# Pass two of a fused expert stage starts from the weights that pass one left, two engines' programs of it become loops, and the steps of a channel norm are spread over more slots

## The chip, the cores and the metric

One core of one Trainium2 chip runs the whole program. The metric is device time in microseconds (us) from start to end of one execution. The engines are TensorE (PE, its weight loads PEld), VectorE (DVE), ScalarE (ACT), GpSimd (POOL) and SyncE (SP, which only issues transfers here). Each runs its own program in order; they meet through semaphores only.

## The reference, cut to what matters

One decoder layer for 512 prompt tokens and 32 decode tokens (544 in all), all in float32. The parts that the change touches:

```python
def conv_branch(u_ext, conv_w, conv_b, conv_norm_g):
    c = lax.conv_general_dilated(u_ext, conv_w[:, None, :], (1,), 'VALID', ...) + conv_b
    return jax.nn.silu(rms_norm(c, conv_norm_g))

def peer_ffn(x, w_query, keys1, keys2, expert_u, expert_v):
    ...                    # idx: 16 of 16384 experts for each of 8 heads, g: their softmax
    act = jax.nn.gelu(jnp.einsum('nd,nhkd->nhk', xc, expert_u[idx]), approximate=False)
    return jnp.einsum('nhk,nhkd->nd', g * act, expert_v[idx])
```

Block-sparse attention over paged caches runs beside the convolution. `expert_u` and `expert_v` are 64 MB each.

## The kernel before

The work comes in stages: the input projection, the attention stage (with the convolution's steps between it), the output and query projections, and two passes over the experts.

**Attention stage.** It runs in slots t = 0 to 64. `at = t - 33` counts the slots of its second half, in which TensorE multiplies one chunk of cached values (1 MB) in each slot (`attend`, L1722), for a first batch of four sequences in `at` 0 to 15 and for a second one in 16 to 31. One unit of prompt attention enters in most slots: scores on TensorE (L1635), maximum on VectorE (L1146, L1148), exponent on ScalarE (L803), norm on VectorE (L1155, L1157), transposes and values on TensorE. Before the second batch, TensorE turns that batch's probabilities in five groups (L1709), and ScalarE copies each group out (`keep_probabilities`, L848 and L851), after it has copied the first batch's output (`keep_output`, L857). TensorE waits at its third group for the first copy. The convolution's RMS norm has these steps: root on ScalarE (L704) in `at` 13, reciprocal (L1020) and four scalings (L1269) on VectorE in `at` 14, four sigmoids `sig_c` (L894) on ScalarE in `at` 15, and the products `finish_conv` (L1235 and after) in `at` 17 to 20. Every value chunk has one of four buffers and is loaded again when an `attend` has freed it.

**Weights of the experts.** A product in float32 is made of three matmuls with a high and a low part. For one step of 256 experts a raw 1 MB tile is loaded (SyncE), ScalarE writes its high part (`high_u`, L922) and another engine the low part (`split_u`). There are three places for split tiles: 0 and 1 (`w_hi`, `w_lo`), and 2, the first 256 columns of `x_hi` and `x_lo`, which are free when pass one is over.

**Pass one** (L1828 and after, `up`) goes over 64 steps for the first 256 tokens; GpSimd makes the low parts (L632). Its activations go to memory, from where single ones are fetched later. The gates of the other tokens are made beside it and stored too.

**Pass two, the fused stage.** 68 slots (`ENDS`). In slot s TensorE does `up_beside` for the other 288 tokens (48 matmuls, with expert step s), and from slot 4 on `down` for expert step s - 4 (48 matmuls, L1525 to L1527 with `a_hi`), whose weights v lie in place 1. Its program is straight for eight slots and then a loop of eight. For the first 256 tokens, whose experts are sparse, GpSimd fetches 256 times one activation per token (`fetch_unit`, L649) and 256 times one row of v per token (`fetch_row`, L656), and VectorE adds the rows (`add_row`, L1430); a row has one of six buffers, so that fetch k + 6 waits for `row_used` of add k. In most slots GpSimd makes four such pairs, and in some five. In the middle of them it multiplies the slot's two activation tiles by the gates (`gate_acts`, L644). ScalarE then makes their high part (`high_a`, L977) and after that the high part of v (`high_v`, L970), VectorE the low parts (`low_acts` L1472, `split_v` L1480, `split_u` L1455), in the order of these loops:

```python
                if c >= 0:
                    split_v(c)
                for k in mine[:1]:
                    add_row(k)
                if slot + 1 < STEPS:
                    split_u(STEPS + slot + 1)
                for k in mine[1:4]:
                    add_row(k)
                for step in gated_at(slot):
                    low_acts(step)
```

`gated_at` gives slot 2 the gates of slots 0 and 1, slot 3 those of 2 and 3, and later each slot its own. GpSimd's first unit fetches wait for the last activations of pass one to be stored.

## Time and profile before

| | |
|---|---|
| median of three runs | 1965.66 us (1964.97 to 1965.74) |
| profiled execution | 1983.77 us, its span 1982.3 us |
| attention stage, second half | about 315 to 436 us of the span |
| pass one | about 617 to 1065 us |
| pass two | 1065 us to the end |
| TensorE's clock, mean over the span | 0.964 of full speed |

The profiled execution is 18.1 us longer than the median of the others. Times inside it are counted from the span's start. A releaser behind "<-" is what ended an idle stretch of an engine, by the semaphore events; "issue" is time that the profile lays to no wait.

### The profile page before, as it was taken

Reading aid. Unit: us, or ns where it says so; the run is one execution under the profiler, and the core shown is the slowest. Engines: PE = TensorE matmul, PEld = TensorE weight load, DVE = VectorE, ACT = ScalarE, POOL = GpSimd, SP = SyncE. Lnnn points to the kernel's source line nnn. Section 1 sums busy time; section 2 is a strip of 40 time slices with the busy share of each in tenths; the row PEclk is TensorE's granted clock in tenths of the full one; section 3 lists DMA queues with packets and bytes.
Section 4 is the critical chain, followed back from the end, with each engine's and each line's share of the span. In section 5 each row is a group of like instructions: output and inputs, shape, how many; then the busy total and the mean of one; then the engine's idle time right before and its main releaser. Section 6 shows DMA issues by size and latency. Waiting matters only on the chain.

```text
span 1982.3 us, 38018 instructions
## 1 busy us (share of the span) xinstructions
PE 1844.2 (93%) x14571; PEld 1732.4 (87%) x14571; DVE 1458.1 (74%) x2603; ACT 821.3 (41%) x1103; POOL 1162.8 (59%) x943
## 2 busy tenths in 40 slices
PE   6988988789899999999998899999999999999996
PEld 6977764349899999999998899999998999999985
DVE  3659675431589889857774788888887888888873
ACT  4233764422213545456774434334333444334331
POOL 3232222223234888874466688888887788888840
PEclk9989998889899999999999899999999999999997
DMA  4353877672123676775687799999999899999971
GB/s 158 87 112 120 287 253 260 230 279 84 65 86 120 216 235 218 221 231 218 234 335 274 242 342 343 349 329 335 340 330 340 308 347 346 341 331 345 320 241 67
DMA packets 207753, 491.59 MB, mean 248 GB/s; under 512 B 34209, under 2 KB 119266, under 8 KB 187138
## 3 DMA queue, kind: packets, MB, share of 16 engines
q1 hardware_dynamic: 145906, 319.11, 46.8%
q0 software_dynamic: 55296, 167.94, 23.7%
q10 hardware_dynamic: 6416, 2.78, 1.1%
q8 instruction: 79, 1.29, 0.3%
q14 instruction: 56, 0.46, 0.1%
HBM read 449.10 MB, written 40.66 MB: 247 GB/s over the span
## 4 chain that ended last, share of the span: by engine, by line
PE 46%; POOL 31%; issue 9%; DVE 7%; ACT 5%; DVEq 1%; DMA 1%; another core or an unknown queue 0%; ACTq 0%; POOLq 0%; SPq 0%
POOL v_rows L656 13%; POOL picked_a L649 12%; PE pair L1525 11%; PE pair L1526 11%; PE pair L1527 11%; POOL act L644 5%; PE pair L1858 3%; PE pair L1670 3%; PE pair L1682 1%; PE pair L1722 1%; PE pair L1535 1%; PE pair L1808 1%; DVE pair L1430 1%; ACT w_hi L970 1%; PE pair L1635 1%
## 5 line engine op out<-in xcount | busy, mean ns | idle before, releaser
L1525 PE MATMUL pair<-x_hi,w_hi 128*128 128x256 f32 (+2 forms) x2048 | 602.4, 294 | 30.9 <-DVE x_lo L1036 13.7
L1526 PE MATMUL pair<-x_lo,w_hi 128*128 128x256 f32 (+2 forms) x2048 | 593.8, 290 | 2.2 <-issue 2.2
L1527 PE MATMUL pair<-x_hi,w_lo 128*128 128x256 f32 (+2 forms) x2048 | 592.5, 289 | 0.1
L1525 PEld LDWEIGHTS pair<-x_hi,w_hi 128*128 128x128 f32 x2048 | 392.7, 192 | 34.1 <-issue 23.2
L1526 PEld LDWEIGHTS pair<-x_lo,w_hi 128*128 128x128 f32 x2048 | 392.4, 192 | 2.9 <-issue 2.7
L1527 PEld LDWEIGHTS pair<-x_hi,w_lo 128*128 128x128 f32 x2048 | 391.2, 191 | 1.0 <-issue 1.0
L656 POOL DMA_INDIRECT v_rows<-in_v_t,at_row x256 | 289.5, 1131 | 109.9 <-issue 75.8
L1430 DVE SCALAR_TENSOR_TENSOR pair<-v_rows,share,pair 128x1024 f32<-128x1024 f32 x254 | 327.3, 1289 | 23.2 <-issue 0.4
L1525 PE MATMUL pair<-a_hi,w_hi 128*128 128x288 f32 x1024 | 312.6, 305 | 30.3 <-DVE w_lo L1480 24.7
L649 POOL DMA_INDIRECT picked_a<-acts_sparse,at_unit x256 | 289.0, 1129 | 74.5 <-issue 68.9
L1527 PE MATMUL pair<-a_hi,w_lo 128*128 128x288 f32 x1024 | 307.6, 300 | 1.5 <-issue 1.5
L1526 PE MATMUL pair<-a_lo,w_hi 128*128 128x288 f32 x1024 | 307.5, 300 | 0.6 <-issue 0.6
L632 POOL TENSOR_TENSOR w_lo<-w_raw,w_hi 128x1024 fp32r<-128x1024 f32 x86 | 204.4, 2399 | 90.5 <-ACT w_hi L922 90.5
L977 ACT ACTIVATE a_hi<-act 128x288 fp32r<-128x288 f32 x128 | 56.5, 444 | 447.9 <-POOL act L644 365.7
L616 POOL TENSOR_TENSOR w_lo<-w_raw,w_hi 128x2048 fp32r<-128x2048 f32 x22 | 101.4, 4610 | 237.5 <-ACT w_hi L713 237.5
L1525 PEld LDWEIGHTS pair<-a_hi,w_hi 128*128 128x128 f32 x1024 | 196.9, 192 | 41.9 <-DVE w_lo L1480 24.5
L1527 PEld LDWEIGHTS pair<-a_hi,w_lo 128*128 128x128 f32 x1024 | 197.1, 193 | 2.2 <-issue 2.2
L1526 PEld LDWEIGHTS pair<-a_lo,w_hi 128*128 128x128 f32 x1024 | 197.3, 193 | 0.0
L1525 PE MATMUL pair<-x_hi 128*128 128x288 f32 x512 | 153.3, 299 | 3.5 <-issue 1.8
L1527 PE MATMUL pair<-x_hi,x_lo 128*128 128x288 f32 x512 | 153.2, 299 | 0.8 <-issue 0.7
L1526 PE MATMUL pair<-x_lo,x_hi 128*128 128x288 f32 x512 | 153.0, 299 | 0.6 <-issue 0.4
L922 ACT ACTIVATE w_hi<-w_raw 128x2048 fp32r<-128x2048 f32 x74 | 141.2, 1908 | 0.0
(221 smaller groups left out, 3381.3 us busy)
## 6 DMA issues: line engine op xcount, KB each, us to landing
w_raw<-in_u_t SPq DMA_DIRECT2D x74, 1024.0 KB, 5.3
v_raw<-in_u_t SPq DMA_DIRECT2D x54, 1024.0 KB
w_raw<-in_v_t SPq DMA_DIRECT2D x128, 256.0 KB
v_raw<-in_v_t SPq DMA_DIRECT2D x128, 256.0 KB
gates<-g_out SPq DMA_DIRECT2D x9, 2048.0 KB, 9.3
g_in<-gates SPq DMA_DIRECT2D x16, 1152.0 KB
v_ring<-in_cache_v SPq DMA_DIRECT2D x64, 256.0 KB, 4.0
v_ring<-in_cache_v POOLq DMA_DIRECT2D x64, 256.0 KB, 4.7
```

The costliest lines, as they stand in the source:

```text
L616: pool.tensor_tensor(w_lo[:, chunk % 2, :], w_raw[:, chunk % 2, :], w_hi[:, chunk % 2, :].bitcast(F32), ALU.subtract).then_inc(w_split, 1)
L632: pool.tensor_tensor(lows[w][:, :, cols], by_blocks(u_raw[u_buffer(t)])[:, :, cols], highs[w][:, :, cols].bitcast(F32), ALU.subtract).then ...
L644: pool.tensor_tensor(mine, mine, g_in[:, slot, :, GCHUNK * tile:GCHUNK * (tile + 1)], ALU.mult)\
L649: pool.indirect_dma_start(picked_a[:, k:k + 1], None, every_unit[:, :], bass.IndirectOffsetOnAxis(ap=at_unit[:, k:k + 1], axis=0))\
L656: pool.indirect_dma_start(v_rows[:, k % RING, :], None, every_row[:, :], bass.IndirectOffsetOnAxis(ap=at_row[:, k:k + 1], axis=0))\
L922: sc.activation(into, by_blocks(u_raw[u_buffer(t)]), ACT.Copy).then_inc(u_hi_done, 1)
L1430: v.scalar_tensor_tensor(total, row, share[:, k:k + 1], total, ALU.mult, ALU.add).then_inc(row_used, 1)
L1525: te.matmul(out, s_hi, m_hi, start=start, stop=False)
L1526: te.matmul(out, s_hi, m_lo, start=False, stop=False)
L1527: return te.matmul(out, s_lo, m_hi, start=False, stop=stop)
L1670: last = te.transpose(bank(PAGE_TURN[j % 2])[:, P * pr:P * (pr + 1)], pages_in[chunk % 4][:, j, P * pr:P * (pr + 1)], ident[:, :])
L1858: last = te.matmul(bank(TURN + g % 2)[:, P * t:P * (t + 1)], hot1[:, piece, TOK * (g % 2) + t, :], hot2[:, piece, TOK * (g % 2) + t, :], s ...
```

## The change

**One.** Pass two takes the expert steps in another order. Slots 0 and 1 use steps 62 and 63, whose split tiles still lie in places 0 and 1; slot 2 uses step 61, whose raw tile still lies in its buffer, and slot 3 step 60, which is loaded at pass one's end. Steps 0 to 59 follow in slots 4 to 63, and v in the same order. Two loads of 1 MB, two high parts, one low part on GpSimd and one on VectorE fall away. **Two.** ScalarE's and SyncE's programs of the stage are written out for slots 0 to 7, are a loop of six rounds for 8 to 55, and written out for 56 to 67; in the loop waits compare with a register's value, and loads have an address from a register. **Three.** In the attention stage the reciprocal becomes two halves in `at` 14 and 15, the scalings two pairs in 16 and 17, the sigmoids come in `at` 18 (behind a copy of output and probabilities that stays in 15), and `finish_conv` in 20 to 23.

```diff
+def step_of(slot):
+    return (STEPS - 2, STEPS - 1, STEPS - 3, STEPS - 4)[slot] if slot < BESIDE else slot - BESIDE
+def tile_of(slot):
+    return 2 * ((2, 3, 1, 0)[slot] if slot < BESIDE else slot % 4)
...
 def place_of_u(step):
-    return 2 * (step % 2)
+    return 1 if step == 1 else 2 * (step % 2)
...
             for t in range(STEPS):
                 wait_low_u(sp, t)
                 if t + 3 < STEPS:
                     load_u(t + 3)
-                else:
-                    (lambda: load_u(STEPS), lambda: load_v(0), lambda: load_u(STEPS + 1))[t + 3 - STEPS]()
+                elif t == STEPS - 2:
+                    load_v(0)
+                elif t == STEPS - 1:
+                    load_u_beside(3)
...
-            wait_low_u(sp, STEPS)
-            load_u(STEPS + 2)
...
+            def load_beside(slot, it=0):
                 c = slot - BESIDE
                 if 0 <= c < STEPS - 2:
-                    sp.wait_ge(v_lo_done, c + 1)
-                    load_v(c + 2)
-                if slot + 3 < STEPS:
-                    wait_low_u(sp, STEPS + slot + 1)
-                    load_u(STEPS + slot + 3)
+                    sp.wait_ge(v_lo_done, 8 * it + c + 1)
+                    load_v(c + 2, 2 * it)
+                if 1 <= slot < STEPS - 3:
+                    sp.wait_ge(u_lo_vector, 16 * it + 2 * slot)
+                    load_u_beside(slot + 3, 8 * it)
...
                 if at == 15:
+                    keep_output(0)
+                    keep_probabilities(1)
+                if at == 18:
                     sc.wait_ge(z_done, 1)
                     for cc in range(CC):
                         sc.activation(sig_c[:, cc, :], conv[:, cc, :], ACT.Sigmoid).then_inc(sigc_done, 1)
-                    keep_output(0)
-                    keep_probabilities(1)
...
+            def beside(slot, it=0):
+                if 1 <= slot < BESIDE:
+                    high_u_beside(slot + 1)
+                elif slot >= BESIDE:
+                    high_v(slot - BESIDE, it)
                 if slot < STEPS:
-                    gelu_out(STEPS + slot, 0)
-                if slot + 1 < STEPS:
-                    high_u(STEPS + slot + 1)
+                    gelu_beside(slot, 0, it)
+                if BESIDE <= slot < STEPS - 1:
+                    high_u_beside(slot + 1, it)
                 if slot < STEPS:
-                    gelu_out(STEPS + slot, 1)
+                    gelu_beside(slot, 1, it)
                 for step in gated_at(slot):
-                    high_a(step)
+                    high_a(step, it)
+
+            for slot in range(8):
+                beside(slot)
+            with sc.Fori(0, STEPS // 8 - 2) as it:
+                for slot in range(8, 16):
+                    beside(slot, it)
+            for slot in range(STEPS - 8, ENDS):
+                beside(slot)
...
-                if at == 14:
-                    reciprocal_rms(rootc_done)
-                    for cc in range(CC):
+                if at in (14, 15):
+                    cols = slice(HALF * (at - 14), HALF * (at - 13))
+                    v.wait_ge(rootc_done, 1)
+                    v.reciprocal(rstd[:, cols], rstd[:, cols])
+                if at in (16, 17):
+                    v.drain()
+                    for cc in range(2 * (at - 16), 2 * (at - 15)):
                         last = v.scalar_tensor_tensor(conv[:, cc, :], conv[:, cc, :], conv_g[:, cc:cc + 1], rstd[:, :],
                                                       ALU.mult, ALU.mult)
-                    last.then_inc(z_done, 1)
-                if 17 <= at < 17 + CC:
-                    finish_conv(at - 17)
+                    if at == 17:
+                        last.then_inc(z_done, 1)
+                if 20 <= at < 20 + CC:
+                    finish_conv(at - 20)
...
-                if slot + 1 < STEPS:
-                    split_u(STEPS + slot + 1)
+                if 1 <= slot < STEPS - 1:
+                    split_u(slot + 1)
...
-            up(STEPS)
-            for slot in range(1, BESIDE):
-                up_beside(STEPS + slot, place_of_u(slot))
+            for slot in range(BESIDE):
+                up_beside(slot, place_of_u(slot), slot < 2)
```

VectorE's rows at the end of `at` 13 and in `at` 14 and 15 stood so (`rstd` is the root's result, `conv` and `conv_g` the channels and their gains, and `stats` and `p_nat` belong to prompt units):

```order
L1148 TENSOR_REDUCE stats<-pair 128x1
L1020 RECIPROCAL rstd<-rstd 128x544 [waits rootc_done]
L1269 SCALAR_TENSOR_TENSOR conv<-conv,conv_g,rstd 128x544 x4
L1165 CAST x_hi<-pair 128x128 [waits pv_done]
L1167 TENSOR_TENSOR x_lo<-pair,x_hi 128x128
L1155 RECIPROCAL stats<-stats 128x1 [waits pe_done]
L1157 TENSOR_SCALAR p_nat<-p_nat,stats 128x384
L1146 TENSOR_TENSOR pair<-pair,causal 128x128 [waits ps_done]
```

They now stand so:

```order
L1173 TENSOR_REDUCE stats<-pair 128x1
L1294 RECIPROCAL rstd<-rstd 128x272 [waits rootc_done]
L1190 CAST x_hi<-pair 128x128 [waits pv_done]
L1192 TENSOR_TENSOR x_lo<-pair,x_hi 128x128
L1180 RECIPROCAL stats<-stats 128x1 [waits pe_done]
L1182 TENSOR_SCALAR p_nat<-p_nat,stats 128x384
L1171 TENSOR_TENSOR pair<-pair,causal 128x128 [waits ps_done]
```

The second half of the reciprocal and the four scalings have moved behind the maximum of the unit that enters in `at` 15. ScalarE's rows from that unit's exponent on stood so (`s_turned` is TensorE's word that a group of probabilities is turned, `z_done` VectorE's that the channels are scaled):

```order
L803 ACTIVATE p_nat,stats<-pair,stats 128x512 [waits pt_done,pm_done]
L894 ACT_TABLE_LOAD
L894 ACTIVATE sig_c<-conv 128x544 [waits z_done]
L894 ACTIVATE sig_c<-conv 128x544 x3
L857 ACTIVATE o_nat<-pair 128x512 [waits o_done]
L848 ACTIVATE pages_pt<-pair 128x512 [waits s_turned] x4
```

They now stand so:

```order
L816 ACTIVATE p_nat,stats<-pair,stats 128x512 [waits pt_done,pm_done]
L870 ACTIVATE o_nat<-pair 128x512 [waits o_done]
L861 ACTIVATE pages_pt<-pair 128x512 [waits s_turned] x4
L864 ACTIVATE own_pt<-pair 32x128 [waits s_turned]
L825 ACTIVATE p_tr<-pair 128x384 [waits pv_done,pt_done]
```

The sigmoids and their table load now stand eight rows further down, in `at` 18. One slot of ScalarE's fused stage was this (`act` are a slot's activations, `x_hi` and `w_hi` the places of high parts):

```order
L977 ACTIVATE a_hi_116<-act_118 128x288 [waits gated] x2
L970 ACTIVATE w_hi<-w_raw 128x2048 [waits down_done,v_loaded0]
L952 ACTIVATE act_118<-pair 128x288 [waits up_done]
L922 ACTIVATE x_hi<-v_raw_115 128x8x256 [waits up_done,u_loaded0]
L952 ACTIVATE act_118<-pair 128x288 [waits up_done]
```

In the loop it is this (from the second `high_a` of a slot, with full names):

```order
L992 ACTIVATE a_hi_0_116<-act_0_118 128x288 [waits gated]
L980 REGISTER_ALU
L982 REGISTER_ALU [waits v_loaded0]
L985 ACTIVATE w_hi_53<-w_raw_52 128x2048 [waits down_done]
L960 REGISTER_ALU
L967 ACTIVATE act_0_118<-pair0 128x288 [waits up_done]
L934 REGISTER_ALU
L937 ACTIVATE x_hi_50<-v_raw_3_115 128x8x256 [waits up_done,u_loaded0]
L960 REGISTER_ALU
```

The activations and their order are the same, with one or two register instructions ahead of most waits. GpSimd's rows differ in one thing only: the two `w_lo` rows of its last `split_u` are gone.

## Rows read from the trace of the kernel before

**Rows 1.** The page: the span
```profile
span 1982.3 us, 38018 instructions
```

**Rows 2.** The page: the chain that ended last, by engine
```profile
PE 46%; POOL 31%; issue 9%; DVE 7%; ACT 5%; DVEq 1%; DMA 1%; another core or an unknown queue 0%; ACTq 0%; POOLq 0%; SPq 0%
```

**Rows 3.** Windows: us, busy (instructions) by engine, PEclk, DMA share, GB/s
```profile
1140.00:1160.00 20.00, 20.00 (x152) 20.00 (x152) 17.34 (x18) 8.63 (x10) 16.20 (x15) 1.00 0.86 302
1200.00:1300.00 100.00, 97.96 (x721) 95.98 (x720) 86.59 (x95) 38.69 (x45) 82.26 (x78) 1.00 0.97 344
```

**Rows 4.** The chain in one slot of pass two: start, us, what
```profile
1243.64 1.58 POOL act L644 x2
...
1247.96 1.62 POOL picked_a L649
...
1252.59 1.77 POOL v_rows L656
...
1256.87 1.58 POOL act L644 x2
```

**Rows 5.** ScalarE in the same slot: start, us, instruction, idle before it
```profile
1245.25 0.45 ACT L977 ACTIVATE a_hi<-act 128x288 fp32r<-128x288 f32 x1 [0.33 <-POOL act L644]
1245.60 1.90 ACT L970 ACTIVATE w_hi<-w_raw 128x2048 fp32r<-128x2048 f32 x1
```

**Rows 6.** VectorE in the same slot
```profile
1247.54 2.36 DVE L1480 TENSOR_TENSOR w_lo<-w_raw,w_hi 128x1024 fp32r<-128x1024 f32 x2 [0.62 <-issue]
1251.18 2.35 DVE L1455 TENSOR_TENSOR x_lo<-v_raw,x_hi 128x1024 fp32r<-128x1024 f32 x2
```

**Rows 7.** The chain in the attention stage
```profile
367.74 3.55 DVE rstd L1020
...
371.37 0.79 DVE conv L1269
...
375.65 0.70 DVE stats L1148
...
376.38 0.78 ACT p_nat L803 x2
...
377.18 1.28 ACT L894
...
378.47 2.29 ACT sig_c L894 x4
```

**Rows 8.** TensorE there: turns, then `attend` of `at` 16 and 18
```profile
381.79 2.20 PE L1709 MATMUL pair<-ident,s_nat 128*128 128x128 f32 x9 [9.81 <-ACT pages_pt L848]
384.59 1.93 PE L1722 MATMUL pair<-v_ring,pages_pt 128*32 128x512 f32 x8 [0.61 <-ACT own_pt L851]
...
393.69 1.06 PE L1722 MATMUL pair<-v_ring,pages_pt 128*32 128x512 f32 x8
```

**Rows 9.** Windows there, columns as in rows 3
```profile
386.00:392.00 6.00, 6.00 (x23) 2.34 (x19) 1.61 (x5) 2.55 (x4) 1.08 (x2) 0.51 0.48 176
```

**Rows 10.** GpSimd at the start of pass two: first of sixteen unit fetches, and gates
```profile
1068.00 0.96 POOL L649 DMA_INDIRECT picked_a<-acts_sparse,at_unit  x1 [5.44 <-DMA acts_sparse<-act_out]
...
1090.92 2.29 POOL L644 TENSOR_TENSOR act<-act,g_in 128x288 f32<-128x288 f32 x3
```

**Rows 11.** TensorE's first matmul of slot 4 of pass two
```profile
1110.67 0.61 PE L1525 MATMUL pair<-x_hi,w_hi 128*128 128x288 f32 x1 [4.14 <-DVE w_lo L1455]
```

**Rows 12.** The chain's longest pieces: two that no instruction fills
```profile
1079.79 6.48 issue
...
1528.29 7.31 another core or an unknown queue
```

**Rows 13.** SyncE's loops over value pages: register and branch instructions, ns
```profile
L454 SPq FUSED_REGOPS  x6: 59/66/73, 315.2 to 413.1; - x6
L454 SPq COMPARE_BRANCH  x6: 40/45/45, 328.8 to 423.7; - x6
```

**Rows 14.** The page: issues, KB, us from issue to landing
```profile
v_ring<-in_cache_v SPq DMA_DIRECT2D x64, 256.0 KB, 4.0
```

More of the change, by code:

```diff
@@ L92, in alone, with u_buffer, u_loads @@
     engine.sem_inc(ready, 1)
-def on_vector(t):
-    return t > STEPS
-def splits_until(t):
-    mine = sum(1 for n in range(t + 1) if on_vector(n))
-    return mine if on_vector(t) else t + 1 - mine
-def u_buffer(t):
-    return t % 3 if t < STEPS else 1 - t % 2
-def u_loads(t):
-    return sum(1 for n in range(t + 1) if u_buffer(n) == u_buffer(t))
+def step_of(slot):
+    return (STEPS - 2, STEPS - 1, STEPS - 3, STEPS - 4)[slot] if slot < BESIDE else slot - BESIDE
+def tile_of(slot):
+    return 2 * ((2, 3, 1, 0)[slot] if slot < BESIDE else slot % 4)
+def u_buffer(slot):
+    return 1 - slot % 2
+def u_loads(slot):
+    return 20 + slot // 2 if slot % 2 == 0 else 21 + (slot + 1) // 2
 def v_loads(c):
@@ L532, in _, with load_gates @@
             by_tiles = gates.rearrange("c p (g i) t -> g p c (i t)", i=8)
-            def load_gates(quad, half):
-                sp.dma_start(g_in[:, half, :, :], by_tiles[quad]).then_inc(g_loaded[half], 16)
+            def load_gates(n, later=0):
+                quad = n - 1 if n else STEPS // 4 - 1
+                sp.dma_start(g_in[:, n % 2, :, :], by_tiles[quad + later]).then_inc(g_loaded[n % 2], 16)
             load_u(0)
@@ L665, in fetch_ahead @@
                     fetch_row(k + RING)
-            for t in range(STEPS + 1):
+            for t in range(STEPS):
                 split_u(t)
@@ L981, in _ @@
             for t in range(STEPS):
-                high_u(t + 1)
+                if t + 1 < STEPS:
+                    high_u(t + 1)
                 groups = gate_groups(t)
@@ L1838, in up @@
                         te.wait_ge(qh_kept, 2 * PH - 1 + t)
-                    wait(te, gelu_done, 2 * t + j - (1 if beside else 2))
-                    made = bank(j if beside else up_bank_of(t, j))[:, 0:tokens.stop - tokens.start]
+                    wait(te, gelu_done, 2 * t + j - 2)
+                    made = bank(up_bank_of(t, j))[:, 0:FIRST]
                     for kd in range(KD):
@@ L1888, in turn_rows, with up_beside @@
                 last.then_inc(rows_turned, 1)
-            def up_beside(t, place):
+            def up_beside(slot, place, prepared=False):
                 for j in range(2):
-                    te.wait_ge(u_lo_vector, 2 * (t - STEPS) - 1 + j)
-                    te.wait_ge(gelu_done, 2 * t + j - 1)
+                    if not prepared:
+                        te.wait_ge(u_lo_vector, 2 * slot - 3 + j)
+                    te.wait_ge(gelu_done, 2 * slot + 2 * STEPS + j - 1)
                     cols = slice(P * j, P * (j + 1))
```

113 lines of the change are left out of this document (57 added, 56 removed).

## The prediction

> **What bounds the kernel now.** I read the page first, then the chain of waits, then windows and single rows where the change works. The page gives a span of 1982.3 us [rows 1]; the profiled execution took 1983.77, 18.1 more than the median. The chain by engine [rows 2] lays 46% to TensorE and 31% to GpSimd: some long stretch hangs on GpSimd, and a change to TensorE's or ScalarE's work there is worth only what it gives to GpSimd.
>
> That stretch is pass two. In its steady part TensorE has 152 matmuls in 20 us when it never waits, and 721 in 100 us over eight slots [rows 3]. A slot has 96 matmuls, so TensorE would need 96 x 20 / 152 = 12.63 us and takes about 13.3. The chain of one slot goes from gates at 1243.64 to gates at 1256.87 [rows 4], 13.23 us, and its pieces are GpSimd's. What returns to GpSimd from the others is indirect: the gates end at 1245.22, `high_a` starts at 1245.25 and `high_v` at 1245.60 [rows 5], `split_v` at 1247.54, `split_u` at 1251.18 [rows 6], and GpSimd's fetches beside them last 1.62 and 1.77 us, where a fetch alone lasts 0.95 or so [rows 4, 10]. So a slot is a closed ring: later `high_v` means later splits, the lengthened fetches later, the gates of the next slot later. A delay of ScalarE there can cost its full size in each slot. That is what the loop of part two must be measured by.
>
> The other place is `at` 14 to 16 of the attention stage. TensorE stands idle for 9.81 us ahead of the turns at 381.79 [rows 8], so since 371.98. The chain in that gap [rows 7]: the reciprocal 3.55 from 367.74, four scalings from 371.37, the next unit's maximum at 375.65, its exponent at 376.38, a table load 1.28 and four sigmoids 2.29, to 380.76; the copy of the output and the first group of probabilities fill the 1.03 to 381.79. Behind it the granted clock is 0.51 [rows 9], the lower of TensorE's two levels, 1.2 GHz, after a gap of nearly ten microseconds; `attend` takes 1.93 there, and 1.06 at 393.69 [rows 8], where the clock is full.
>
> **Part three, the norm's steps spread.** VectorE: half the reciprocal, 1.78, and four scalings of some 0.72 (the first has 0.79 [rows 7]) leave the way of the next unit's maximum: 4.7 us. The exponent would start at 371.7; I take 372.85, because TensorE's work up to 371.98 contains scores and transposes that the same unit's steps on VectorE stand behind. ScalarE: exponent 0.8 (376.38 to 377.18), no table load, no sigmoids, then the 1.03: TensorE starts at about 374.6, 7.1 earlier. The gap shrinks from 9.8 to 2.6 us. From 381.79 to 384.59 the turns ran slowly; I take 1.2 us of those 2.8 back at a higher clock, so `attend` of `at` 16 starts 8.3 earlier, and of the further 9.1 us up to 393.69, nearly all at 0.51, I take 2.4 back (at most half, 4.5; but part of them are waits on ScalarE and VectorE). Sum 10.7, bounds 7.1 (the clock falls all the same) and 12.8.
>
> That gain must live to the end of the stage. Nothing behind it has a fixed date except the loads of values, 1 MB for each `attend`, each started when an earlier one frees a buffer; the best windows move 344 GB/s [rows 3], so twelve chunks need 12 x 1.05 MB / 344 = 36.6 us, and the rest of the stage has about 50. I take no loss, and keep one as a rival. The reciprocal's second half and the scaling pairs now stand on VectorE in `at` 15 to 17, each under 1.8 us and behind the unit's own steps. Behind the sigmoids in `at` 18 (1.28 + 2.29, and the exponent's table again, another 1.28 [rows 7]: 4.85 on ScalarE) wait the next unit's exponent and copies. The prompt units run more than a slot ahead of what TensorE needs of them, which covers most of it; I take 0.7 as cost, bounds 0 and 2.5, half of the 4.85. Part three: -10.0.
>
> **Part one, pass two's start.** TensorE has two slots ready, so the waits of slot 1 for `split_u` go, 1 to 2 us. But what sets slot 4 is GpSimd: sixteen unit fetches from 1068.00, 1.25 apart, then fetched rows and the gates of slots 0 and 1 at 1090.92 [rows 10], then those of 2 and 3, and only behind them on ScalarE's program `high_v(0)`, on which `split_v(0)` and the first `down` wait. None of these is shortened, and `high_u` of slot 4 stands behind the `high_a` of slot 2, so TensorE arrives earlier and waits longer. TensorE's first matmul of slot 4 was at 1110.67 after 4.14 of waiting [rows 11]. The 2 MB fewer loads are hidden, since GpSimd waits for none of them. I take -1, bounds +1 (a longer wait, and a clock that falls in it: of the first 6 us behind it no more than 1 beyond what falls already) and -2. The profiled execution has here a piece of 6.48 us that no instruction fills, and one of 7.31 at 1528.29 [rows 12]. The slot of the second has the same program as its neighbours, which don't show it. I take both as accidents of this execution: they are 13.8 of the 18.1 by which it exceeds the median. So the sum is made against it with its own stalls taken out, 1970.0, and the remaining 4.3 are small accidents too.
>
> **Part two, the loops.** The order of the activations is kept. Added on ScalarE are about five register instructions in each looped slot, 48 slots, and five taken back-edges. The trace has no loop on ScalarE; the nearest rows are SyncE's, 0.066 for a register instruction and 0.045 for a branch [rows 13]. In the ring only the pair ahead of `high_v` counts, 0.13 per slot, and it is worked off while `high_a` runs (0.45 long, with 0.35 from start to start [rows 5]). So 0, with 0.13 x 48 = 6.3 as upper bound. For a back-edge the bounds are 0.045 and, if code has to come from memory, one load's 4.0 us [rows 14]; SyncE's loops, six rounds in 95 to 98 us, show nothing of such a size in their rows, so I take 0.3, near the lower: 5 x 0.3 = +1.5, bounds 0.2 and 20. SyncE's own loop issues loads that have two slots of time; cover gone, it would cost as much per round, but it has over 20 us.
>
> The Trainium skill, "Runtime: NRT & Kernel Launch", section "Instruction fetch mechanics", says that a taken branch whose target isn't in the current window of two pages forces a DMA fetch of it before execution goes on, and that a page holds 256 instructions. ScalarE's body has about 109 instructions, so by that rule the target mostly lies in the window and the sum stays; where it crosses a page, the rule gives a stall at each back-edge. No row before shows such a stall on ScalarE.
>
> **Sum.** -10.0 - 1.0 + 1.5 = -9.5. Profiled: 1983.8 - 9.5 = 1974.3 if its accidents came again; median: 1965.66 - 9.5 = 1956.2, which I round to 1956. The likeliest case's own range is 1952 to 1960.
>
> **Rivals.**
> *A: the stall at 1079.79 is no accident.* For it: 6.48 us lie just where TensorE, ScalarE and SyncE wait for each other over u's tiles, which part one removes. Against: the time of the other runs. Then part one gives 6.5 more, up to 1965.7 - 9.5 - 6.5 = 1950, and with the clock behind it about 1946. Chance 0.12.
> *B: the loop costs.* ScalarE's pair of register instructions is in the ring, 6.3, and each back-edge waits for its code, 5 x 4.0 = 20: +26.3 in place of +1.5 gives 1981. It decides from 14.9 us added (11.0 gained plus the bound of 3.9 for no change), which is 0.31 per looped slot or 3.0 per back-edge. For it: the ring has no slack. Against: the 0.35 pitch hides the pair. By the skill's rule named above this would come if the body straddled pages at every round. Chance 0.07, slower in 0.05.
> *C: the attention gap is filled again.* The turns come earlier, but the clock stays low and the sigmoids of `at` 18 with two table loads make TensorE wait for a unit, or the value loads become the bound: 7.1 - 2.5 - 1 or so, 3 to 5 us kept. Then 1965.7 - 4 = 1962, at the edge of no change. For it: 4.85 us of ScalarE now stand among prompt units; against: units ahead. Chance 0.14, half of it within the bound.
> *D: the ring loosens.* The longer fetches sit where splits overlap them; a small shift of `split_u` past a fetch takes 1.77 back to 1.0 or so. Then slots fall to TensorE's 12.63: up to 0.6 x 50 = 30, and I would put it at 20 to 25, 1933. For it: the ring depends on an alignment. Against: the order on VectorE and GpSimd is unchanged in the loop. Chance 0.05.
>
> **The numbers.** 0.62 for the forecast, 0.12 A, 0.07 B, 0.14 C, 0.05 D. A measurement tells a change from none by about 0.2%, 3.9 us: no change is 1961.7 to 1969.6. The range 1944 to 1963 takes in A, the forecast and most of C, and leaves out B, D and the rest of C, some 0.17. Faster: 0.62 + 0.12 + 0.07 + 0.05 = 0.86; same: 0.07 of C and 0.02 of B, 0.09; slower 0.05.
>
> **What would show it.** Part three: TensorE's idle ahead of the turns 2 to 4 us and not 9.8; `attend` of `at` 16 about 8 us earlier with about 1.06 each; the stage's end 8 to 11 earlier. A wait on `p_nat` after `at` 18 above 2 us would be C. Part one: no stall in slots 0 to 2, TensorE's wait ahead of slot 4 longer (7 or so), its start within 2 us of where it was, counted from pass two's start and without the 6.48. Part two: gates of neighbouring slots 13.2 apart as before; at a back-edge of ScalarE (once in eight slots) under 0.5 between its instructions. A pitch of 13.4 or more, or 4 us at a back-edge, makes it wrong on the slow side; a pitch of 12.7 on the fast side.

## The result, and the profile after

The changed kernel takes 1952.33 us (median of five runs, 1950.15 to 1956.25), the one before 1964.97 beside it: ratio 0.9937, 95% interval 0.9923 to 0.9952, so 12.4 us less (9.4 to 15.1). The forecast was 1956 and faster.

The page's span, to set beside [rows 1]:

```profile
span 1948.5 us, 38904 instructions
```

That is 33.8 us less than the profiled execution before, nearly three times the change of the medians. So the two traces can't just be subtracted, and I followed one landmark after another. In the attention stage TensorE's rows, from the turns on, answer to [rows 8] (start, us, engine, line, operation, count, idle before it and its releaser):

```profile
369.23 1.15 PE L1739 MATMUL pair<-ident,s_nat 128*128 128x128 f32 x8 [1.92 <-ACT pages_pt L861]
...
371.22 1.06 PE L1752 MATMUL pair<-v_ring,pages_pt 128*32 128x512 f32 x8 [0.36 <-ACT own_pt L864]
...
376.92 1.06 PE L1752 MATMUL pair<-v_ring,pages_pt 128*32 128x512 f32 x8
```

The window behind it, with the columns of [rows 3], answers to [rows 9]:

```profile
372.00:378.00 6.00, 6.00 (x42) 2.68 (x39) 3.82 (x8) 1.87 (x4) 2.15 (x4) 1.00 0.66 221
```

The idle time fell from 9.81 to 1.92 us, the granted clock is full, and `attend` takes 1.06 and not 1.93. GpSimd's first low part of pass one ends the stretch. It started at 619.13 and now at 602.67. Counted from TensorE's `attend` of `at` 15 (367.37 and 362.70), that is 251.8 and 240.0: 11.8 us gained. Of these, 10.8 are there at the `attend` of `at` 27 (54.10 us behind that of `at` 15 before, 43.28 now). The other 4.7 were gained ahead of that `attend`, where the programs are the same, 2.4 of them before the first value chunk. Those are the execution's own. The last `attend` of the stage waited for its load of values before and still does:

```profile
430.89 1.93 PE L1722 MATMUL pair<-v_ring,pages_pt 128*32 128x512 f32 x8 [1.29 <-DMA v_ring<-in_cache_v]
```

```profile
414.88 1.94 PE L1752 MATMUL pair<-v_ring,pages_pt 128*32 128x512 f32 x8 [1.11 <-DMA v_ring<-in_cache_v]
```

The wait has not grown, so the loads followed the lead and did not eat it.

At the start of pass two, GpSimd's first unit fetch and TensorE's first matmul of slot 4 answer to [rows 10, 11]:

```profile
1050.76 0.96 POOL L662 DMA_INDIRECT picked_a<-acts_sparse,at_unit  x1 [14.68 <-DMA acts_sparse<-act_out]
...
1082.55 0.61 PE L1555 MATMUL pair<-x_hi,w_hi 128*128 128x288 f32 x1 [6.24 <-DVE w_lo L1485]
```

Slot 4 starts 31.8 us behind that fetch, and 42.7 before. On GpSimd itself, the first unit fetch to the twenty-ninth takes 66.7 us and took 76.3. The ring behind it is as it was. GpSimd's rows of a slot answer to [rows 4]:

```profile
1220.96 1.62 POOL L662 DMA_INDIRECT picked_a<-acts_sparse,at_unit  x1 [0.30 <-issue]
...
1225.60 1.76 POOL L669 DMA_INDIRECT v_rows<-in_v_t,at_row  x1 [0.52 <-issue]
...
1256.50 1.58 POOL L657 TENSOR_TENSOR act<-act,g_in 128x288 f32<-128x288 f32 x2
...
1269.73 1.57 POOL L657 TENSOR_TENSOR act<-act,g_in 128x288 f32<-128x288 f32 x2
```

The pitch of the gates (from those of one slot to those of the next) is 13.23 us in most slots with four pairs of fetches in both traces; a few, near the start and in the middle, have 12.6. The piece of 7.31 us at 1528.29 [rows 12] is gone and doesn't come back in any of the twelve profiles below.

### The profile page after: what moved, and what is told of

It reads as the page before. It is cut to its first block, busy times and chain, and to the rows that moved or that the text cites. A ratio compares the mean times of both kernels' runs of the same rounds, so it can differ in the third digit from the quotient of the medians.

```text
span 1948.5 us, 38904 instructions
## 1 busy us (share of the span) xinstructions
PE 1823.1 (94%) x14571; PEld 1719.4 (88%) x14571; DVE 1456.1 (75%) x2602; ACT 817.2 (42%) x1101; POOL 1159.0 (59%) x941
## 3 DMA queue, kind: packets, MB, share of 16 engines
q8 instruction: 79, 1.29, 0.3%
## 4 chain that ended last, share of the span: by engine, by line
PE 45%; POOL 32%; issue 8%; DVE 8%; ACT 4%; DVEq 2%; DMA 1%; ACTq 0%; SPq 0%; POOLq 0%
POOL v_rows L669 13%; POOL picked_a L662 13%; PE pair L1555 11%; PE pair L1556 11%; PE pair L1557 11%; POOL act L657 5%; PE pair L1887 3%; DVE conv L1105 3%; PE pair L1700 2%; PE pair L1712 1%; ACT w_hi L985 1%; PE pair L1838 1%; PE pair L1752 1%; PE pair L1565 1%; DVEq L1454 1%
## 5 line engine op out<-in xcount | busy, mean ns | idle before, releaser
L1555 PE MATMUL pair<-a_hi,w_hi 128*128 128x288 f32 x1024 | 313.0, 306 | 38.9 <-DVE w_lo L1510 37.8
L645 POOL TENSOR_TENSOR w_lo<-w_raw,w_hi 128x1024 fp32r<-128x1024 f32 x84 | 199.6, 2398 | 85.9 <-ACT w_hi L931 85.9
L1555 PE MATMUL pair<-x_hi 128*128 128x288 f32 x496 | 146.5, 295 | 2.4 <-DVE x_lo L1485 2.4
L1557 PE MATMUL pair<-x_hi,x_lo 128*128 128x288 f32 x496 | 146.9, 296 | 0.0
L1556 PE MATMUL pair<-x_lo,x_hi 128*128 128x288 f32 x496 | 146.5, 295 | 0.0
L645 POOL TENSOR_TENSOR w_lo<-v_raw,w_hi 128x1024 fp32r<-128x1024 f32 x44 | 104.7, 2400 | 60.6 <-ACT w_hi L931 60.6
```

The costliest lines, as they stand in the source:

```text
L645: pool.tensor_tensor(lows[w][:, :, cols], by_blocks(u_raw[t % 3])[:, :, cols], highs[w][:, :, cols].bitcast(F32), ALU.subtract).then_inc(u ...
L1555: te.matmul(out, s_hi, m_hi, start=start, stop=False)
L1556: te.matmul(out, s_hi, m_lo, start=False, stop=False)
L1557: return te.matmul(out, s_lo, m_hi, start=False, stop=stop)
```

## The experiments

e1 to e5 and e11 take the change and its places apart, the others test what the ring is made of. Ratios are against the kernel before on the same chip, with 95% intervals; 0.001 is 2 us.

| kernel | ratio | interval | median us |
|---|---|---|---|
| changed kernel | 0.9937 | 0.9923 to 0.9952 | 1952.3 |
| e1 part three alone | 0.9966 | 0.9951 to 0.9980 | 1957.1 |
| e2 parts one and two | 0.9993 | 0.9981 to 1.0006 | 1964.4 |
| e3 changed, no loops | 0.9942 | 0.9922 to 0.9961 | 1953.2 |
| e4 sigmoids moved alone | 1.0000 | 0.9988 to 1.0013 | 1965.6 |
| e5 changed, copies first | 0.9909 | 0.9893 to 0.9924 | 1949.2 |
| e6 changed, splits in quarters | 0.9865 | 0.9845 to 0.9885 | 1940.7 |
| e7 changed, high_v first | 0.9888 | 0.9870 to 0.9907 | 1944.1 |
| e8 changed, a delay on ScalarE | 0.9946 | 0.9929 to 0.9963 | 1954.9 |
| e9 copies first and quarters | 0.9857 | 0.9837 to 0.9877 | 1937.0 |
| e10 changed, splits whole | 1.0296 | 1.0270 to 1.0323 | 2021.6 |
| e11 before, early tile | 0.9990 | 0.9978 to 1.0002 | 1963.4 |
| e12 copies, quarters, high_v first | 0.9745 | 0.9726 to 0.9765 | 1915.9 |

On the three chips of the experiments the kernel before had medians of 1965.8, 1968.7 and 1965.3 and its times spread over 12.5, 6.8 and 8.9 us, far more than the 1.6 beside the changed kernel. The changed kernel itself was not run again there, so what an experiment gains on it compares two ratios. A gain of 2 or 3 us is therefore read from the traces here, not from the times.

### The parts apart

e1 is the kernel before with the hunks of part three; e2 is the changed kernel with them taken back.

> The kernel before with part three alone (reciprocal in halves, scalings in pairs, sigmoids in slot 18). Gap theory: all but one or two us of the gain sits in the attention stage; the profile of the changed kernel shows its second batch of values 11.4 us earlier than before, counted from the value multiply of at 15. So 1965 - 11 = 1954 (1952.5 to 1955.5), TensorE's wait ahead of the turns about 2 us and the clock at its upper level behind them. Rival, the start of pass two gives most of it (9.5 us between the two profiles): this kernel then gains only 3 to 4 us, 1961.

> Parts one and two without part three: the attention stage as before. Gap theory with the stall as an accident: gain of 1 to 2 us, 1963.5 (1962.5 to 1964.5), and the first down of pass two no more than 2 us earlier in an execution whose chain holds no empty piece of 6 us. Rival, the stall of 6.48 us at the start of pass two is the old order's own and present in every run: gain of 8 to 10 us, 1956.

e1 gained 6.7 us by its ratio (3.9 to 9.6), short of 11. Its trace says why. TensorE's rows and the window behind the turns:

```profile
369.58 2.20 PE L1715 MATMUL pair<-ident,s_nat 128*128 128x128 f32 x9 [1.92 <-ACT pages_pt L848]
372.38 1.93 PE L1728 MATMUL pair<-v_ring,pages_pt 128*32 128x512 f32 x8 [0.60 <-ACT own_pt L851]
```

```profile
372.00:378.00 6.00, 5.62 (x18) 2.12 (x19) 0.74 (x2) 0.82 (x3) 1.08 (x2) 0.50 0.40 135
```

The gap is 1.92 us as in the changed kernel, whose program is the same there, and yet the granted clock is 0.50, the level of 1.2 GHz. The stretch from `attend` of `at` 15 to pass one took 241.7, a gain of 10.1. But only 6.7 of it are there at the `attend` of `at` 27 (47.39 us behind that of `at` 15, 54.10 before), and the rest came behind it, where the programs are the same. The 6.7 agree with the time. e2 has the old stage (251.6 us there) and gained nothing that its time can tell (1.4 us, -1.2 to 3.7), but its GpSimd took 66.8 us from the first unit fetch to the twenty-ninth.

e3 writes the two loops out:

```diff
-            with sc.Fori(0, STEPS // 8 - 2) as it:
+            for it in range(STEPS // 8 - 2):
```

> The changed kernel with ScalarE's and SyncE's programs of the fused stage written out, no loop (parts one and three stay). The gates of the changed kernel are 13.37 to 13.40 us apart where ScalarE's loop turns back and 13.24 elsewhere, so the theory says the loops cost 5 x 0.15 = 0.8 us: this is 0.5 to 1 us faster, 1951.5, and no gap of 13.37 is left. Rival: a back-edge sometimes waits for its code, and that is why the five times of the changed kernel spread over 6.1 us (1950.15 to 1956.25) where those of before spread over 1.6: then this one has times within 1.5 us of each other, near 1950.

The times can't tell the two apart (0.9942 and 0.9937). The trace shows the pitches of 13.37 gone: the slots that had them are 13.21 to 13.26. The rival is down: its ten times lie between 1946.6 and 1959.4, so the spread isn't the loop's. What a back-edge costs shows on ScalarE in the changed kernel; the branch stands between these two instructions at 1244.8, and they are 0.52 apart from start to start, where [rows 5] has 0.35:

```profile
1244.71 0.45 ACT L992 ACTIVATE a_hi<-act 128x288 fp32r<-128x288 f32 x1 [0.31 <-POOL act L657]
1245.23 1.92 ACT L985 ACTIVATE w_hi<-w_raw 128x2048 fp32r<-128x2048 f32 x1
```

That is 0.17 us, and the slot's pitch is 13.40. At the other four back-edges it is 0.12 to 0.14 on ScalarE and 0.14 to 0.15 in the pitch, so about 0.7 us for all five. No wait of the 4.0 us of a load shows.

e4 moves only the sigmoids and the products `finish_conv`, and leaves the reciprocal and the scalings whole in `at` 14.

> The kernel before with only ScalarE's half of part three: sigmoids and their products moved to slots 18 and 20, reciprocal and four scalings left whole in slot 14. TensorE's gap ahead of the turns loses the 3.6 us of table load and sigmoids and keeps VectorE's 4.7: gap of about 6 us. Theory that lengths add: 3.6 us earlier plus perhaps 1 of the slow clock, 1960.5. Rival, the clock decides: a gap of 6 us still brings the lower clock, so 1961.5 and the granted clock near 0.5 behind it; or the clock stays high already, then 1958.

```profile
374.19 2.20 PE L1710 MATMUL pair<-ident,s_nat 128*128 128x128 f32 x9 [6.21 <-ACT pages_pt L848]
376.99 1.93 PE L1723 MATMUL pair<-v_ring,pages_pt 128*32 128x512 f32 x8 [0.60 <-ACT own_pt L851]
...
383.16 1.94 PE L1723 MATMUL pair<-v_ring,pages_pt 128*32 128x512 f32 x8
```

The gap lost its 3.6 us to the digit (6.21 for 9.81), the clock stayed at its lower level (0.50 in 380 to 384), and the stage from `attend` 15 to pass one took 249.9 us, 1.9 less. The time shows nothing. Where the rest of the 3.6 went, two later rows tell, the `attend` of `at` 21 and of `at` 24, first in the profile before, then in e4:

```profile
403.63 1.06 PE L1722 MATMUL pair<-v_ring,pages_pt 128*32 128x512 f32 x8
...
413.63 1.06 PE L1722 MATMUL pair<-v_ring,pages_pt 128*32 128x512 f32 x8
```

```profile
396.81 1.06 PE L1723 MATMUL pair<-v_ring,pages_pt 128*32 128x512 f32 x8
...
408.08 1.06 PE L1723 MATMUL pair<-v_ring,pages_pt 128*32 128x512 f32 x8
```

The stretch between them takes 10.00 us before and 11.27 here. It takes 10.00 or 10.01 in e2 and e11, which have the old stage too, and 11.26 to 11.28 in every kernel with the sigmoids and products moved. So that move costs 1.3 us behind the turns, out of the 3.6 that it takes from the gap. With that the lengths add up. At the `attend` of `at` 27, e4 is 2.3 to 2.4 us ahead of e2 and e11 (and 1.5 ahead of the profile before, whose clock rose 0.8 us earlier than theirs). Against that profile, e1's 6.7 are 7.9 of gap and 0.1 behind it, less 1.3; the changed kernel's 10.8 are 7.9 of gap, 0.8 in the turns and 3.4 in the next two `attend`s at the full clock, less 1.3.

### The toss of the clock

e5 puts the copies that TensorE waits for ahead of ScalarE's exponent:

```diff
+                if t - FIRST_VALUES == 15:
+                    keep_output(0)
+                    keep_probabilities(1, range(2))
                 if t in started:
                     prompt_exp(started[t])
...
                 if at == 15:
-                    keep_output(0)
-                    keep_probabilities(1)
+                    keep_probabilities(1, range(2, 5))
```

> The changed kernel with the output's copy and the first two groups of probabilities ahead of the exponent of at 15 on ScalarE, which is idle there for 1.66 us. TensorE's wait of 1.92 us ahead of the third group of turns is what stays of the gap: behind it the granted clock was 1.00 in the changed kernel and 0.50 in the kernel with the spread norm alone, whose attention stage has the same program, and its batch was 3.9 us longer. Theory that a gap of 1.9 us is a toss for the clock: with the gap under 0.6 us the clock stays high always; gain 1.3 us on executions that had a high clock and 5 on the others, so 2 to 4 us below the changed kernel's 1952.3, near 1949.5. Rival, the wait moves on to the next unit's exponent, later by 1 us, and the stage ends where it did: 1952.

```profile
371.19 0.28 PE L1741 MATMUL pair<-ident,s_nat 128*32 128x128 f32 x1 [0.50 <-ACT pages_pt L861]
371.83 1.06 PE L1754 MATMUL pair<-v_ring,pages_pt 128*32 128x512 f32 x8 [0.36 <-ACT own_pt L864]
```

The wait of 1.92 is gone, and the six runs lie within 3 us at 1949.2. Over all profiles with the spread norm: with the gap of 1.92 us the clock stayed up in four (the changed kernel, e3, e8, e10) and fell in three (e1, e6, e7); with the copies first (e5, e9, e12) it stayed up in all three. `attend` 16 to 17 takes 3.3 us where it stayed up and 5 to 6.2 where it fell. From `attend` 15 to `attend` 27 it is 43.3 us in the four, 45.7 to 47.4 in the three that fell, and 41.9 with the copies first; to pass one it is 240.0 to 240.4, 241.7 to 243.6, and 238.6 to 240.5. So the toss is worth 2.5 to 4.1 us in the stage, and the copies first give 1.4 by themselves. Three profiles without a fall prove little, since four in seven held with the gap as well. The ratio of e5 is 0.0028 under that of the changed kernel, and their intervals just touch: that it is faster is likely, not settled. The toss can be only part of the spread of the times, since e3's ten lie 12.8 us apart; the rest is not explained.

### Why slot 3 was late

e11 is the kernel before with one load moved:

```diff
+            wait_low_u(sp, STEPS + 1)
+            load_u(STEPS + 3)
             load_v(1)
             load_gates(1, 1)
```

> The kernel before with one move: the load of slot 3's u tile, which was issued at 1071.27 behind nine other transfers and their waits and landed at 1082.16, is issued before the loads of v and of the second gates. In the kernels with the old order TensorE waits about 8 us ahead of slot 3 and GpSimd takes 70.4 us from its first unit fetch to its twenty-ninth, in those with the new order 66.7. Theory: that late tile is what part one removes, so the tile lands by 1075, GpSimd's stretch falls to 67 or 68, and the time by 2 to 3.5 us. Rival, it is the work left out (two high parts, a split) that gives the 3.7: the stretch stays at 70.

First ScalarE, VectorE, TensorE and GpSimd in e4, whose start of pass two is the old one; then SyncE in e11 and TensorE's first matmul of slot 3:

```profile
1082.18 1.91 ACT L923 ACTIVATE x_hi<-v_raw 128x2048 fp32r<-128x2048 f32 x1 [3.64 <-DMA v_raw<-in_u_t]
...
1084.12 5.41 DVE L1456 TENSOR_TENSOR x_lo<-v_raw,x_hi 128x1024 fp32r<-128x1024 f32 x2 [6.54 <-ACT x_hi L923]
...
1089.59 0.61 PE L1526 MATMUL pair<-x_hi 128*128 128x288 f32 x1 [8.29 <-DVE x_lo L1456]
...
1091.19 0.94 POOL L656 DMA_INDIRECT v_rows<-in_v_t,at_row  x1 [1.94 <-DVE pair L1431]
...
1098.09 1.05 POOL L644 TENSOR_TENSOR act<-act,g_in 128x288 f32<-128x288 f32 x1 [0.69 <-ACT act L953]
```

```profile
1067.42 0.54 SPq L517 DMA_DIRECT2D v_raw<-in_u_t  x1
1068.01 3.55 SPq L523 DMA_DIRECT2D v_raw<-in_v_t  x4
1071.61 1.70 SPq L535 DMA_DIRECT2D g_in<-gates  x1
```

```profile
1083.24 0.40 PE L1527 MATMUL pair<-x_hi 128*128 128x288 f32 x1 [1.50 <-DVE x_lo L1457]
```

In the old order the tile's load was issued at 1071.27, behind six others of a queue that had waited for the stored gates until 1066.5, and landed 10.9 us later. ScalarE's high part was late by 3.64. VectorE's split began at 1084.12, just ahead of GpSimd's four gate multiplications (from 1084.29), and took 5.41 us instead of 2.36; the row that VectorE adds behind it came late, and GpSimd waited 1.94 us for a free row buffer. Up to the gates of slot 4 its waits for row buffers, beyond the usual 0.30, come to 4.6 us, and to 2.1 in e11. TensorE's slot 3 was late by 8.29, so GpSimd waited 0.69 for its activations too, and not in e11. The two make 3.2 of the 3.7 us. Moved ahead, the load shortens the wait of 8.29 to 1.50, and GpSimd's stretch to the twenty-ninth fetch takes 66.7 us (1061.76 to 1128.48) in place of 70.4, all that part one brings, with none of its work left out. TensorE's slot 4 comes 31.9 us behind the first fetch, 31.8 in the changed kernel and 38.9 in e4. The time agrees, 0.9990, but can't prove it alone.

### What the ring is made of

e8 adds a tiny activation, 0.20 us long, ahead of the second `high_a`, into unused cells:

```diff
+                    if j:
+                        sc.activation(stats[:, 64 + 4 * (slot % 8):68 + 4 * (slot % 8)], act[slot // 4 % 2][:, tile, 0:4],
+                                      ACT.Copy)
                     sc.activation(a_hi[slot // 4 % 2][:, tile, :], act[slot // 4 % 2][:, tile, :], ACT.Copy)\
```

> The changed kernel with one more tiny activation (128x4, into unused cells) ahead of the second high_a of every slot, which delays high_v by about 0.2 us in each of 64 slots: the price of rival B by itself. Theory of the ring as predicted: the delay goes whole into each slot, pitch 13.24 + 0.2, and 60 slots make it 10 to 13 us slower than the changed kernel, 1964. Rival, the delay moves split_v past the start of a fetch, or is taken up by GpSimd's own pace: pitch 13.24 or less, 1952.

ScalarE and, in the next two rows, GpSimd's gates of two neighbouring slots:

```profile
1220.53 0.20 ACT L993 ACTIVATE stats<-act 128x4 f32<-128x4 f32 x1 [0.31 <-POOL act L657]
1220.64 0.43 ACT L995 ACTIVATE a_hi<-act 128x288 fp32r<-128x288 f32 x1
1220.97 1.90 ACT L985 ACTIVATE w_hi<-w_raw 128x2048 fp32r<-128x2048 f32 x1
```

```profile
1218.92 1.58 POOL L657 TENSOR_TENSOR act<-act,g_in 128x288 f32<-128x288 f32 x2
...
1232.24 1.58 POOL L657 TENSOR_TENSOR act<-act,g_in 128x288 f32<-128x288 f32 x2
```

From `high_a` of the first tile to `high_v` it is now 1.20 and was 1.11 (1257.36 to 1258.47): the activation cost 0.09, half of what I had expected. The pitch is 13.32, 0.09 more, in nearly every slot. So the ring passes a delay on whole, and GpSimd takes 5.5 us more from its first unit fetch to its last, not the 10 to 13 of the expectation. The ratio is 0.0009 above the changed kernel's, with intervals that overlap.

e6, e10 and e7 shift or cut VectorE's splits. e6 makes quarters of the halves in `split_u` and `split_v`, e10 one piece of the whole; e7 moves `high_v` ahead of `high_a` and `split_v` ahead of `low_acts`:

```diff
-                for first in (0, KD // 2):
-                    mine = slice(first, first + KD // 2)
+                for first in range(0, KD, KD // 4):
+                    mine = slice(first, first + KD // 4)
```

```diff
                     high_v(slot - BESIDE, it)
+                for step in gated_at(slot - 1):
+                    high_a(step, it)
...
-                for step in gated_at(slot):
-                    high_a(step, it)
```

> The changed kernel with VectorE's splits of pass two in four pieces of 128x512 each, not two of 128x1024. In the traces a fetch of GpSimd that starts inside one piece of a split ends 0.80 us after the end of that piece (split_v 1220.55, its first piece to 1221.78, fetch from 1220.96 to 1222.58; split_u's second piece to 1226.56, fetch to 1227.36), and one that starts outside lasts 0.94. Theory: a fetch waits for the end of the piece in which it starts, so pieces of 0.6 us bring the two lengthened fetches from 1.62 and 1.77 to 1.4 or less, the pitch of the gates falls from 13.24 to TensorE's own 12.6 to 12.8, and 50 slots give 20 to 30 us: 1927. Rival, a fetch must wait for the whole split, or the four pieces catch more fetches and lengthen VectorE's own chain: pitch 13.2 or more, 1952 or slower.

> The changed kernel with each split of pass two as one piece of 128x2048: the other direction from quarters. By the rule that a fetch of GpSimd ends 0.80 us after the piece in which it starts, the fetch that begins 0.41 us into split_v now ends 0.8 behind 2.35 us and not 1.2: 1.1 us more per slot, and split_u may catch one as well; one instruction less saves VectorE 0.1. Pitch 14.0 to 14.5, about 55 us slower than the changed kernel, 2005. Rival, it is VectorE's own length, or the count of pieces that costs GpSimd: then pitch 13.2 or less, 1950.

> The changed kernel with high_v ahead of high_a on ScalarE and split_v ahead of low_acts on VectorE (both take the activations of the slot before). high_v then waits for TensorE's down instead of GpSimd's gates, and split_v starts some 2 us earlier in GpSimd's slot. Theory of the ring: what counts is where a split's piece meets a fetch, so the pitch may change either way; by the rule that a fetch ends 0.80 after the piece in which it starts, the first fetch behind the gates starts as split_v does, and a later one is caught for about 1 us: pitch 13.2 to 13.4, 1950 to 1958. At the start of pass two the first split_v no longer stands behind the gates of slots 2 and 3: TensorE's wait ahead of slot 4 falls, but GpSimd's chain isn't shortened by it, nothing gained. Rival, any earlier high_v shortens the ring: pitch 12.7, 1930.

In the changed kernel a split took 2.36 us in two pieces (L1510 and L1485):

```profile
1220.55 2.36 DVE L1510 TENSOR_TENSOR w_lo<-w_raw,w_hi 128x1024 fp32r<-128x1024 f32 x2 [0.62 <-ACT w_hi L985]
...
1224.20 2.36 DVE L1485 TENSOR_TENSOR x_lo<-v_raw,x_hi 128x1024 fp32r<-128x1024 f32 x2
```

With whole splits, VectorE and GpSimd in one slot:

```profile
1222.79 2.29 DVE L1510 TENSOR_TENSOR w_lo<-v_raw,w_hi 128x2048 fp32r<-128x2048 f32 x1 [0.62 <-ACT w_hi L985]
...
1226.37 2.28 DVE L1485 TENSOR_TENSOR w_lo<-w_raw,w_hi 128x2048 fp32r<-128x2048 f32 x1
```

```profile
1223.20 2.69 POOL L662 DMA_INDIRECT picked_a<-acts_sparse,at_unit  x1 [0.30 <-issue]
1226.20 0.94 POOL L669 DMA_INDIRECT v_rows<-in_v_t,at_row  x1 [0.30 <-issue]
1227.45 2.02 POOL L662 DMA_INDIRECT picked_a<-acts_sparse,at_unit  x1 [0.30 <-issue]
```

The splits end at 1225.08 and 1228.65, and the two fetches that began inside them end at 1225.89 and 1229.47: 0.81 and 0.82 us behind. The fetch at 1226.20, begun 0.17 ahead of its split, has its 0.94. The rule from the changed kernel's rows holds to 0.02 us here. In all of e10's trace between 1110 and 1860 us, 103 fetches began inside a split, and each ended 0.80 to 0.84 us behind it; the other 321 lasted 1.03 at most. The pitch is 14.35, as expected (14.0 to 14.5); the loss of 69 us by the medians is more than the 55 that I had put down, because all of some 60 slots pay and not the 50 that I had counted, and those that had a pitch of 12.6 now pay 1.8. With quarters:

```profile
1225.36 1.10 POOL L662 DMA_INDIRECT picked_a<-acts_sparse,at_unit  x1 [0.30 <-issue]
...
1230.17 1.31 POOL L669 DMA_INDIRECT v_rows<-in_v_t,at_row  x1 [1.22 <-issue]
```

The long fetches fell from 1.62 and 1.76 to 1.10 and 1.31. The pitch fell to 12.88, not to 12.6. What takes the place of the long fetches are waits for a row buffer, here what GpSimd's row fetches waited for between 1200 and 1860 us (us in total, times, longest), first in the changed kernel, then with quarters:

```profile
POOL v_rows L669 <- DVE pair L1460: 2.1, 3, 0.7
```

```profile
POOL v_rows L669 <- DVE pair L1460: 66.0, 57, 1.7
```

VectorE, with four pieces a split, is busy 94% of the time there (87% in the changed kernel) and frees rows later. (The 1.22 above isn't such a wait: that fetch starts 1.31 us behind its add, those that waited for theirs mostly 0.21 to 0.27.) e6 gained 14 us on the changed kernel, where the expectation was 25.

e7 gained 9.6 us on the changed kernel by its ratio: between theory and rival. Its trace has a pitch of 12.9 in some rounds and 13.55 in others, but it can't explain the gain: the profiled execution, 1952.4 us, was the slowest of five (median 1944.1), and in it GpSimd takes 805.6 us from its first unit fetch to its last, no less than the changed kernel's 804.4. Whether the rounds of 13.55 belong to that execution alone is open.

### The versions together

> The changed kernel with both edits that gained: copies ahead of the exponent of at 15, and pass two's splits in quarters. They work in different stages, so their gains should add: 5.5 us (ratio 0.9909 against 0.9937) and 14 us (0.9865). Theory: ratio 0.984, 1935, with the pitch of the gates 12.88 as in the kernel with quarters and a high clock behind the turns. Rival: the quarters' kernel had a low clock in its attention stage and so gained less than it can, or the two share the part that is the chip's; then 0.9865 stays.

> Copies first and quarters as before, and high_v ahead of high_a as well. Pitches were 12.88 with quarters, 12.9 (13.55 in some rounds) with high_v first, 13.24 without either. Theory: with short pieces it matters little where a split meets a fetch, so the earlier high_v adds little: 12.75 to 12.9, between 0 and 5 us faster than copies and quarters alone, 1932. Rival, both take the same 0.35 us, and GpSimd's waits for row_used (1.2 and 1.7 us in the trace with quarters) grow instead: no gain or slower.

e9 came out at 0.9857, 1937.0, with the high clock and the pitch of 12.88: 4 us short of the sum of both gains (0.9837) and 1.6 ahead of its rival (0.9865), and its interval holds both. e12 surprised me. I had expected up to 5 us over e9 and it gave 21: 1915.9 us, 2.55% under the kernel before. Windows of e9 and e12, columns as in [rows 3]:

```profile
1200.00:1300.00 100.00, 97.47 (x722) 96.06 (x722) 94.48 (x125) 36.55 (x42) 73.89 (x77) 1.00 0.96 340
```

```profile
1200.00:1300.00 100.00, 99.85 (x750) 99.62 (x750) 93.83 (x130) 41.66 (x48) 78.62 (x82) 1.00 0.98 354
```

750 matmuls in 100 us are TensorE's own pace within 1.3% (152 in 20 [rows 3]), and the pitch of slots with four pairs lies between 12.0 and 13.3. From 1200 to 1860 us TensorE's matmuls wait 0.2 us for other engines, and 10.0 in e9: GpSimd's chain is no longer the bound and TensorE is. `high_v`, released by TensorE and not by the gates, has cut the ring, and short pieces keep GpSimd's fetches under a slot's length. Either alone gave up to 14 us; both together move the bound.

## Why the prediction was right, step by step

The sign, the range and the first term were right. Its terms, with what was measured:

**Part three, -10.0 (bounds of the gap 7.1 and 12.8).** 10.8 by the `attend` of `at` 27 in the changed kernel, where the clock stayed high, and 6.7 in e1, where it fell (0.8 more each against e2 and e11). The gap came out at 1.9 us and not 2.6, so 7.9 for 7.1. The turns gave 0.8 for 1.2, and the clock behind them 3.4 for 2.4 (9.1 us for two `attend`s before, 5.7 now), but 0 and 0.1 in e1. The sigmoids and products in their new place cost 1.3 for 0.7. The prediction had the low clock as a bound and in a rival, but nothing for a toss between the two.

**Part one, -1 (bounds +1 and -2).** Mis-sized, and outside its bounds: -3.7 by the traces. What failed is the step "the 2 MB fewer loads are hidden, since GpSimd waits for none of them", with "none of these is shortened" ahead of it. GpSimd waits for no load itself. It waits for a row buffer that VectorE frees behind a split and for activations of slot 3, and both stand behind a high part, behind a load that SyncE had queued behind a wait for the gates (e11). A load hidden from the engine that bounds can still reach it over others. That TensorE's wait ahead of slot 4 would grow was right: 4.14 before (2.71 in e4) and 6.24 now. That slot 4 would start within 2 us of where it was, counted from pass two's start and without the 6.48, was not: 36.2 us behind the first fetch by that count, 38.9 in e4, and 31.8 now.

**The two stalls as accidents, 13.8 of 18.1.** The one at 1528 never came back. Of the other, 6.48 ahead of slot 2, the later traces say: with the old order that stretch of GpSimd takes 70.4 to 70.7 us (e4, e1), and took 76.3 in that profile, so 5.6 to 5.9 were this execution's own. But rival A was right about the mechanism: SyncE, ScalarE and TensorE do wait for each other over u's tiles there, at slot 3 and not at slot 2, and it costs 3.7 us or more in both later profiles of the old order. The truth lay between forecast and rival.

**Part two, +1.5.** 0.12 to 0.17 on ScalarE at a back-edge, 0.14 to 0.17 in the pitch, so about 0.7 for five. The register instructions cost nothing, as forecast: [rows 5]'s 0.35 between `high_a` and `high_v` is 0.35 still. Rival B's premise, that the ring has no slack, is shown by e8, and its price is not there. The Trainium skill, "Runtime: NRT & Kernel Launch", section "Instruction fetch mechanics", has a fetch of code only where the target of a taken branch isn't in the current window of two pages. The trace agrees as far as it goes, with at most 0.17 us at a back-edge of 109 instructions; a jump out of the window no run here shows.

**The sum.** -10.8 or -6.7, -3.7 and +0.7 make -13.8 with the high clock and -9.7 with the low one by the traces; the times say -12.4 (-9.4 to -15.1). The forecast of -9.5 lies at the interval's edge, short by part one. With the high clock all three terms erred the same way, by 0.8, 2.7 and 0.8 us; with the low one, part three's error of 3.3 goes the other way and cancels the other two, so there the forecast's number is right by luck.

**Rival D** had the right mechanism for another change: a shift of the splits takes the fetches' extra time back and hands the bound to TensorE. e12 does what it says and is 38 us ahead of the changed kernel by its ratio.

## What to carry to other kernels

Where two engines' instructions lengthen each other, cut the pieces of the one short before you look for its waits: whole, half and quarter splits gave pitches of 14.35, 13.23 and 12.88 us for the same work. A wait for a load isn't hidden because the bounding engine never names the load; follow it through every engine that frees or makes something for it, and look what else its queue had to wait for first. A gap on TensorE has two prices, its length and the slow clock behind it: at 1.92 us the second, 2.5 to 4.1 us here, came in three of seven profiles. And steps that leave a gap have a price where they go: here 1.3 us of the 3.6 that ScalarE's left.

## What the runs showed of the hardware that I had not expected

A gap of 1.92 us on TensorE, with the same program around it, was followed by a granted clock of 1.00 in four profiles and of 0.50 in three. An indirect fetch of GpSimd that starts inside a tensor-tensor piece of VectorE ends 0.80 to 0.84 us behind that piece (all 103 such fetches of e10), in the changed kernel also when the next piece follows at once (`split_v`'s first piece to 1221.78, the fetch to 1222.58); the scalar-tensor-tensor of `add_row`, 1.29 us long, doesn't lengthen it. The other way round, VectorE's split took 5.41 us in place of 2.36 when four multiplications of gates began on GpSimd 0.17 us into it (e4). And an activation of 0.20 us, put between two others, delayed what is behind it by only 0.09.
